# Score units of a recurrent layer in two sets of PSUM banks beside a compression in one bank, and two SBUF buffers moved by 96 bytes

## The reference, cut to what matters

```python
def step(S, inp):                                   # the recurrence, per head
    r_t, w_t, k_t, v_t, a_t, b_t = inp
    sa = jnp.einsum('bhvk,bhk->bhv', S, a_t)
    S = S * w_t[:, :, None, :] + sa[..., None] * b_t[:, :, None, :] + v_t[..., None] * k_t[:, :, None, :]
    return S, jnp.einsum('bhvk,bhk->bhv', S, r_t)

def compress(z, pe, w1, w2):                        # 15 blocks of 32 tokens, stride 16, of 2 heads
    blk = kv_heads(z)[:, cmp_idx] + pe[None, None, :, None, :]
    blk = jnp.transpose(blk, (0, 3, 1, 2, 4)).reshape(B, Hk, n_cmp, CMP_BLOCK * dk)
    return jax.nn.gelu(blk @ w1) @ w2

k_cmp = compress(kc, pe_k, ck1, ck2)
v_cmp = compress(vc, pe_v, cv1, cv2)
```

## Time and profile before

| | us |
|---|---|
| median of three runs | 1469.38 (1469.09 to 1470.21) |
| the profiled execution | 1469.0 |
| its span, first to last instruction | 1467.2 |
| TensorE busy | 1427.4 (97%) |
| VectorE busy | 958.4 (65%) |
| ScalarE busy | 698.3 (48%) |
| GpSimd busy | 86.9 (6%) |

### The profile page before, as it was taken

How to read it: one execution, slowest core, us unless ns; L and a number is a source line. 1 busy time by engine, 2 the same in 40 slices (tenths; PEclk the granted TensorE clock), 3 DMA queues, 4 the chain that set the end, 5 groups by cost and what they waited for, 6 DMA issues and landing times. The chain is left out here.

```text
span 1467.2 us, 26041 instructions
## 1 busy us (share of the span) xinstructions
PE 1427.4 (97%) x10266; PEld 1313.1 (89%) x10266; DVE 958.4 (65%) x1559; ACT 698.3 (48%) x1119; POOL 86.9 (6%) x140
## 2 busy tenths in 40 slices
PE   8998999999999999999999999999999999999998
PEld 7886998899998999989989999999999878899997
DVE  4766657766667766666467666676665667576665
ACT  6763444543345434457564434353433656544342
POOL 2040001000002000010000000010000114000000
PEclk9999999999999999999999999999999999999999
DMA  8343001654553545424336545445545423455440
GB/s 347 142 157 130 1 1 44 244 212 175 186 201 130 216 176 201 180 96 163 130 121 246 193 176 201 182 166 184 205 176 189 161 86 140 149 216 195 172 171 29
DMA packets 26575, 238.06 MB, mean 162 GB/s; under 512 B 2544, under 2 KB 6784, under 8 KB 7808
## 3 DMA queue, kind: packets, MB, share of 16 engines
q1 hardware_dynamic: 23824, 233.39, 43.1%
q10 hardware_dynamic: 2672, 3.58, 0.7%
HBM read 235.89 MB, written 1.07 MB: 162 GB/s over the span
## 5 line engine op out<-in xcount | busy, mean ns | idle before, releaser
L440 PE MATMUL ps<-uT_h,w_gu 128*128 128x256 f32 x3520 | 614.1, 279 | 0.4 <-DVE w_gu L1953 0.4
L440 PEld LDWEIGHTS ps<-uT_h,w_gu 128*128 128x128 f32 x3520 | 537.7, 188 | 11.0 <-issue 1.4
L440 PE MATMUL ps<-uT_l,w_gu 128*128 128x256 f32 x1760 | 478.8, 279 | 0.0
L440 PE MATMUL ps<-w_dn,h_r 128*128 128x512 f32 x1320 | 326.2, 396 | 0.3 <-DVE h_r L1995 0.3
L440 PEld LDWEIGHTS ps<-uT_l,w_gu 128*128 128x128 f32 x1760 | 325.4, 188 | 0.0
L440 PEld LDWEIGHTS ps<-w_dn,h_r 128*128 128x128 f32 x1320 | 239.4, 188 | 51.2 <-issue 1.7
L1303 ACT CAST w_gu<-ring 128x2048 fp32r<-128x2048 f32 x110 | 209.9, 1909 | 154.9 <-PE ps L440 154.8
L1953 DVE TENSOR_TENSOR w_gu<-ring,w_gu 128x2048 fp32r<-128x2048 f32 x110 | 252.1, 2292 | 34.5 <-ACT w_gu L1303 34.1
L1986 DVE TENSOR_TENSOR us<-ps,bc 128x256 f32<-128x256 f32 x110 | 46.5, 422 | 202.6 <-PE ps L440 202.5
L1316 ACT ACTIVATE wk<-wk 128x256 f32<-128x256 f32 x110 | 46.1, 419 | 261.4 <-DVE wk L1984 261.4
L1309 ACT CAST w_dn<-ring 128x1024 fp32r<-128x1024 f32 x110 | 115.6, 1051 | 82.9 <-PE ps L440 82.7
(11 more groups left out here) (385 smaller groups left out, 1789.0 us busy)
## 6 DMA issues: line engine op xcount, KB each, us to landing
ring<-wstream SPq DMA_DIRECT2D x144, 1536.0 KB, 6.2
cst<-consts_in SPq DMA_DIRECT2D x1, 2185.0 KB, 13.7
wk<-t_row ACTq DMA_DIRECT2D x1, 2048.0 KB, 7.8
wk<-masks_in SPq DMA_DIRECT2D x1, 1216.0 KB, 24.0
x<-x_in SPq DMA_DIRECT2D x2, 512.0 KB, 4.6
ring<-wstream SPq DMA_DIRECT2D x1, 1024.0 KB, 8.7
inh<-gains ACTq DMA_DIRECT2D x2, 512.0 KB, 9.5
out_dram<-x SPq DMA_DIRECT2D x3, 256.0 KB, 2.1
```

Source lines behind the costliest of these rows:

```text
L440: return pe.matmul(o, l, r, start=start, stop=stop, skip_group_check=True)
```

## The change

It has four parts. Pairs 3, 5 and 7 write their scores to `ps[6]` and `ps[7]` (`A_bank`), and a pair beyond the third waits for the reads of the pair before the last; the M part of two pairs is issued with the odd one. The compression's two strips both go to `ps[4]`, and one ScalarE copy takes them; the two sets of transposes go one after the other through `ps[5]`, behind m = 2 and m = 8, and ScalarE copies them within `compress`. Pairs 3 to 6 stand one step earlier, and the first level product waits for quad 0 only, while `compress_T` waits for all reads. Last, 96 bytes are left free ahead of `inh`, which move it, `gate_r` and `ring`, and 32 bytes ahead of `ffb`, so that `ffb`, `cst` and `wk` move by 128.

```diff
+        sb("space_w", [P, 24])
         inh = sb("inh", [P, KC * 3 * P])
         gb = inh[:, 0:2 * D].rearrange("p (a b) -> p a b", b=D)
         sb("gate_r", [P, 2 * KC * 24])
         ring = sb("ring", [P, RING, SLOT])
+        sb("space_f", [P, 8])
         ffb = sb("ffb", [P, 4, T])
...
-        A_COMPRESS = {2: 3, 5: 4, 8: 5, 11: 6, 13: 7}
+        A_COMPRESS = {1: 3, 4: 4, 7: 5, 10: 6, 13: 7}
...
+        def A_bank(u):
+            return ps[6 + u % 2] if u // 2 in (3, 5, 7) else ps[u % 2]
...
# TensorE, rwkv_A(p)
-                else:
+                elif p < 3:
                     pe.wait_ge(s["A_read"], 2 * p)
+                elif p > 3:
+                    pe.wait_ge(s["A_read"], 2 * (p - 1))
                 rows_ = [slice(HD * h, HD * (h + 1)) for h in range(2)]
                 for h, r in enumerate(rows_):
-                    mm(ps[h][:, 0:256], bT[r, c, tk], arT[r, c, t, :])
+                    mm(A_bank(2 * p + h)[:, 0:256], bT[r, c, tk], arT[r, c, t, :])
                 for h, r in enumerate(rows_):
-                    mm(ps[h][:, 256:512], kT_[r, c, tk], arT[r, c, t, :]).then_inc(s["A_ps"], 1)
-                if k and p % 2 == 0:
-                    pe.wait_ge(s["M_ready"], k)
-                for h, r in enumerate(rows_):
-                    mm(ps[2 + h][:, p % 2 * P:(p % 2 + 1) * P], arT[r, c, t, 0:P], bT[r, c, tk]
-                       ).then_inc(s["Mm_ps"], 1)
+                    mm(A_bank(2 * p + h)[:, 256:512], kT_[r, c, tk], arT[r, c, t, :]).then_inc(s["A_ps"], 1)
+                if p % 2:
+                    if k:
+                        pe.wait_ge(s["M_ready"], k)
+                    for b in range(2):
+                        for h, r in enumerate(rows_):
+                            ch = c - 1 + b
+                            mm(ps[2 + h][:, b * P:(b + 1) * P], arT[r, ch, t, 0:P], bT[r, ch, tk]).then_inc(s["Mm_ps"], 1)
# TensorE, rwkv
-                pe.wait_ge(s["A_read"], RWKV_UNITS)
+                pe.wait_ge(s["A_read"], RWKV_UNITS - 2)
...
-                    pe.wait_ge(s["M_ready"], max(q + 1, QUADS))
+                    pe.wait_ge(s["M_ready"], max(q + 1, QUADS) if q else 1)
...
-                        pe.wait_ge(s["cmp_row"], 2)
+                        pe.wait_ge(s["cmp_row"], 1)
+                        pe.wait_ge(s["A_read"], RWKV_UNITS)
                         compress_T()
# TensorE, compress
-                        last = mm(ps[4 + n][HD * n:HD * n + 33, 0:256], misc[:, 384 * n + m:384 * n + m + 8 * 32 + 1:8],
+                        last = mm(ps[4][HD * n:HD * n + 33, 0:256], misc[:, 384 * n + m:384 * n + m + 8 * 32 + 1:8],
...
-                rwkv_tok(ps[6], bT, 0)
-                rwkv_tok(ps[7], kT_, 0)
+                    if m == 2:
+                        rwkv_tok(ps[5], bT, 0)
+                    if m == 8:
+                        pe.wait_ge(s["tok_ev"], 3)
+                        rwkv_tok(ps[5], kT_, 0)
# ScalarE: out of rwkv, into compress, ahead of the wait for cmp_h
+                for n in range(2):
+                    act.wait_ge(s["tok_ps"], 3 + n)
+                    A(act.copy(bktok[:, n, :], ps[5][:, :]), "tok_ev")
                 act.wait_ge(s["cmp_h"], 1)
-                for n in range(2):
-                    r = slice(HD * n, HD * n + 33)
-                    A(act.copy(hrow[r, n, :], ps[4 + n][r, 0:T]), "cmp_row")
+                A(act.copy(hrow[0:97, 0, :], ps[4][0:97, 0:T]), "cmp_row")
# VectorE, rwkv
-                    V(v.copy_predicated(Mt[:, u, :], mask(LEVELS), ps[u % 2][:, 0:P]))
-                    V(v.copy_predicated(AA4[k][:, u % 4, :], msk[:, 0:512], ps[u % 2][:, :]), "A_read")
+                    V(v.copy_predicated(Mt[:, u, :], mask(LEVELS), A_bank(u)[:, 0:P]))
+                    V(v.copy_predicated(AA4[k][:, u % 4, :], msk[:, 0:512], A_bank(u)[:, :]), "A_read")
```

More of the change, by code:

```diff
@@ L956, in compress_T @@
                         last = pe.transpose(ps[6 + n][:, half * 48:half * 48 + 33],
-                                            hrow[r, n, half * P:(half + 1) * P], ident[r, r])
+                                            hrow[r, 0, half * P:(half + 1) * P], ident[r, r])
                 last.then_inc(s["cmp_hT"], 1)
@@ L1429, in rwkv @@
             def rwkv():
-                for n in range(2):
-                    act.wait_ge(s["tok_ps"], 3 + n)
-                    A(act.copy(bktok[:, n, :], ps[6 + n][:, :]), "tok_ev")
                 i = 0
```

## The result

The changed kernel takes **1474.58 us** (median of 8, 1474.09 to 1475.14) against 1469.47 for the one before (median of 8): ratio 1.0033, 95% interval 1.0023 to 1.0043. It is slower by 5.1 us where 6.6 less were forecast. The profiled execution spans 1472.4 us.

The account below looks back on a forecast made before the run. TensorE, busy 97% of the span, was taken as the bound, idling 4.70 us in turns with VectorE in the compression stretch. 1469.4 - 4.9 (two bank sets) - 1.7 (addresses) = 1462.8 us; range 1460.5 to 1467.0.

Parts of the forecast that it names:

- Part 1, two sets of banks: In the compression stretch, TensorE and VectorE stop taking turns; second level product at 125.7 instead of 130.66, -4.9 us.
- Part 2, one bank: Both compression halves write bank 4; their strips still run side by side, costed at nothing.
- the rival of 6.7 us: In the compression, one bank serialises the matmuls, +6.7 us, 1469.5 in all; chance 0.05.
- Part 3, the addresses: Moving in_h and ring speeds matmuls in the input projection and the even and odd layers: -1.7 us, bounds 0 and 2.8.
- three stages fit one rule: weights at 0 modulo 128 cost 3.3 ns more: From input projection, FFN and even layer rates: 0.1200, 0.1167 and 0.118 us a matmul; moved weights would run at 0.1167.
- The rival that came true: In the FFNs, wk's move changes its place modulo 256: 5280 matmuls 3.3 ns slower, +17.4 us, 1480.2; chance 0.08.
- The range: For the whole kernel, 1460.5 to 1467.0 us, leaving out both FFN cases and the serialised bank.
- The page that spoke against part 3: For TensorE matmuls, stream and weight load have separate SBUF read ports; by it the addresses give nothing, 1464.5 us.

Follow-up runs that it names:

- e3: The kernel before with wk alone moved by 128 bytes: 1475.65 us, ratio 1.0043.
- e4: The kernel before with 96 bytes ahead of in_h and 160 ahead of ffb (ring and in_h move by 96, ffb and wk by 256): 1469.38 us, ratio 0.9998.
- e7: The changed kernel with 160 bytes instead of 32 ahead of ffb, so wk and ffb keep their place modulo 256: 1464.70 us, ratio 0.9968.
- e1: The changed kernel without its two spacers, so new order and banks with every buffer at its old place: 1465.67 us, ratio 0.9972.
- e5: The kernel before with 128 bytes ahead of in_h, moving in_h, gate_r, ring, ffb, cst and wk by 128: 1478.47 us (single execution).
- e11: The changed kernel without its two spacers, with wk alone moved by 96 bytes (distance 64 modulo 256): 1447.93 us (single execution).
- e9: The changed kernel without its two spacers, with wk alone moved by 32 bytes (distance 0 modulo 256): 1476.59 us (single execution).
- e6: The kernel before with 128 bytes ahead of ffb and 128 more ahead of wk; ring and in_h stay: 1470.10 us (single execution).
- e13: The kernel of e11 once more, timed against the kernel before for an interval: 1446.91 us, ratio 0.9854.
- e15: The changed kernel with 64 bytes ahead of in_h and 64 ahead of ffb, so wk, ring and in_h stand at distance 64: 1443.03 us, ratio 0.9845.

## Why the prediction was wrong, point by point

- **Part 1, two sets of banks: right, a little less.** The mechanism came out as laid out: pairs at 108.8, 112.5, 115.0, 118.7 and 121.2 for the forecast 109.0, 112.5, 115.0, 118.5 and 121.0, VectorE done at 125.6 for 125.3. The order alone measured 4.0 us for 4.9. Most of the missing 0.9 is in the rows: the 0.61 us between the last compression matmul and the first level product, for the wait for `cmp_h` and the three increments that free the ring's slots. They stood in the code in both kernels and were left out of the sum; before, the eight transposes and the 1.12 of waiting for VectorE covered them. (One small slip in the working: 1.27 + 2.16 + 0.06 is 3.49. The measured 3.46 of that pair has 1.24 for its first term, from 110.41 to 111.65.)
- **Part 2, one bank: right.** 8 instructions in 1.09 us as in twos; the rival of 6.7 us fell.
- **Part 3, the addresses: here the forecast failed.** The step was "three stages fit one rule: weights at 0 modulo 128 cost 3.3 ns more". It rested on two places only, 0 and 224 modulo 256 behind `uT`, which are the same modulo 32 but differ modulo 64, 128 and 256; any modulus from 64 up fitted them, and 128 was taken, the one by which the FFN's arena did not move. The FFN was therefore forecast at 0.1167 as before, a change of nothing, and ran at 5.694 / 48 = 0.1186. e3 (128 bytes, +6 us) and e4 (256 bytes, nothing) show 256. The forecast gain did not come either: 1.7 us were counted, and the move with `wk` kept at its place modulo 256 measured 0.3 (e4) and 1.0 (e7 against e1), neither clear of noise. The input projection did get faster, from 0.1198 to 0.1181 on average and not to 0.1167; at 128 behind `uT` (e5), where the rule has 0.1200, it ran at 0.1186. The start of the compression, counted from the projection's first matmul, came 0.7 earlier, of which 0.2 is the M part moved into pair 1. The even and the odd layer's stages lost 0.7 where 0.5 less was forecast.
- **The rival that came true** had 0.08: the move reaches the FFN by a modulus of 256. Its mechanism and its place were right, its price double: it put the worst rate seen (0.1200) on all 5280 matmuls, +17.4; in whole steps they took 2.0 ns more each (94 ns over 48) and the second product 8 ns a step less, 8.9 us in the FFNs. It was given so little because no row spoke for it. But no row could: the trace of before has each buffer in one place. A term of 5280 instructions without a row should have had the even chance of an unknown, not a small one.
- **The range** ended at 1467.0. The one edit without evidence could move 5280 instructions by 3 ns either way, 1445 to 1480, and both ends were seen: 1482 at one place, 1447 at another.
- **The page that spoke against part 3.** The Trainium skill's page "TensorE: Matmul & The Clock Gate", section "Step-by-step: what each phase is for", has the weight load take nothing from the running matmul's reads. From that the prediction took that places don't matter. The runs differ for this shape (fp32r, 128 weight columns, 256 streamed): from 5.466 (e11) to 5.753 us (e9) for the same 48 instructions with nothing moved but `wk`, at a granted clock of 0.998 and 0.999. By which mechanism the two operands meet no run shows, so it stays open whether it is the weight load's reads.

## What to carry to other kernels

A spacer is an edit to every matmul that reads a buffer behind it. Before one adds it, list which pairs of operands change their distance modulo 256 and how many instructions read them; keep the dense pairs by padding to 256, or try all eight places of 32 bytes, each with several executions, since the best one tried was worth nearly five times the scheduling gain (18.7 against 4.0 us). When bank hand-overs are the bound, lay both engines' timelines out as here (the pairs' starts and VectorE's end held to 0.3 us), and then look for the waits and semaphore increments that the removed waits had covered.

## What the runs showed of the hardware that was not expected

- The start distance of back-to-back fp32r matmuls with 128 weight columns and 256 streamed ones lay between 0.1133 and 0.1200 us by the distance of the two SBUF operands modulo 256. In the FFN 224, 0, 32, 64, 96 and 160 gave 0.1167, 0.1199, 0.1183, 0.1139, 0.1174 or 0.1186, and 0.1197 on average over the 48. The second product (512 streamed) moved too, from 0.229 to 0.2345 each, not in step with the first and not by its own operands' distance alone: `w_dn` stands 96 behind `h_r` modulo 256 in e3 and in e6, and the 12 took 2.814 and 2.795.
- One distance can run in several rhythms: 0.1173 and 0.1200 within one stage, 5.466 and 5.653 us a step within one execution. What chooses is open, beyond that a run of matmuls mostly keeps its rhythm. Two single executions of e13 and e15 lay 7.7 and 12 us above their medians; whether those are two and three FFNs in the other rhythm at 3.9 us each was not seen, as neither was profiled.
- The places 128 and 192 were not tried for the FFN.
